# Three edits to a two-layer diffusion block on one core: where two half-matrix sums are rounded, when the late modulation chunks are made, and how the second-matrix tiles of the first MLP are cut into columns

## The reference, cut to what matters

```
def rms_norm(x, g, eps=1e-6):
    xf = x.astype(jnp.float32)
    y = xf * lax.rsqrt(jnp.mean(xf * xf, axis=-1, keepdims=True) + eps)
    return (y * g.astype(jnp.float32)).astype(x.dtype)

def modulate(x, g, shift, scale):
    return rms_norm(x, g) * (1.0 + scale) + shift

def squared_relu_mlp(h, w_in, w_out):
    return jnp.square(jax.nn.relu(h @ w_in)) @ w_out

for i in range(2):                       # DEPTH
    last = i == 1
    ml = jnp.split((silu(c) @ w_mod[i] + b_mod[i])[:, None, :], 6, axis=-1)
    mc = jnp.split(silu(c_ctx) @ w_mod[i] + b_mod[i], 6, axis=-1)
    hl = modulate(xl, norm_mix_g[i], ml[0], ml[1])
    hc = modulate(xc, norm_mix_g[i], mc[0], mc[1])
    # i == 0: Fourier groups + neighbourhood attention; i == 1: differential attention
    yl, yc = mixer_i(hl, hc)
    xl = xl + ml[2] * yl
    xl = xl + ml[5] * squared_relu_mlp(modulate(xl, norm_mlp_g[i], ml[3], ml[4]), w_mlp_in[i], w_mlp_out[i])
    if not last:                         # the context tokens go through the first layer's MLP only
        xc = xc + mc[2] * yc
        xc = xc + mc[5] * squared_relu_mlp(modulate(xc, norm_mlp_g[i], mc[3], mc[4]), w_mlp_in[i], w_mlp_out[i])
return rms_norm(xl, final_norm_g)
```

## Time and profile before

| | us |
|---|---|
| median of 3 runs | 1603.57 |
| lowest and highest run | 1601.69, 1603.67 |
| the profiled execution | 1603.09 |
| its span, first to last instruction | 1601.3 |
| PE busy | 1573.3 |
| DVE busy | 894.1 |
| ACT busy | 604.7 |
| POOL busy | 910.0 |

### The profile page before, as it was taken

The page is one execution under the profiler, slowest core; times in us unless marked ns, Lnnn a source line. Parts: engine busy times, 40 slices in busy tenths (PEclk is TensorE's granted clock), DMA queues, the critical chain, the costliest instruction groups (busy, mean ns, idle before and its releaser), DMA issues.

```text
span 1601.3 us, 24059 instructions
## 1 busy us (share of the span) xinstructions
PE 1573.3 (98%) x9272; PEld 1408.7 (88%) x9272; DVE 894.1 (56%) x1364; ACT 604.7 (38%) x1009; POOL 910.0 (57%) x1103
## 2 busy tenths in 40 slices
PE   8999999999899999999999999999999999999998
PEld 5889988988899999999998888878889878888887
DVE  4696457347845656647556746049965753232234
ACT  4422456325252342442542511248853412222222
POOL 2443475326677768768762656354415865555562
PEclk9999999999999999999999999999999999999999
DMA  8574212212042232333352223110003332323221
GB/s 350 197 268 153 93 41 100 80 48 85 27 157 81 80 119 82 116 115 123 105 182 82 91 78 96 66 43 1 1 12 130 129 126 93 105 92 101 83 93 53
DMA packets 50348, 163.15 MB, mean 102 GB/s; under 512 B 6336, under 2 KB 8768, under 8 KB 46656
## 3 DMA queue, kind: packets, MB, share of 16 engines
q1 hardware_dynamic: 50240, 161.68, 29.4%
HBM read 158.78 MB, written 2.10 MB: 100 GB/s over the span
## 4 chain that ended last, share of the span: by engine, by line
PE 86%; DVE 6%; POOL 2%; issue 2%; DMA 2%; ACT 1%; SPq 0%; POOLq 0%; DVEq 0%; ACTq 0%
PE ps L2109 24%; PE ps L2110 24%; PE ps L2111 24%; PE ps L2748 3%; PE ps L2710 2%; PE ps L2737 1%; PE ps L2615 1%; POOL w_lo L744 1%; PE ps L2603 1%; PE ps L2643 1%; PE ps L2427 1%; DVE mod_acc L1439 1%; DMA mod_big<-w_mod_dram 1%; DVE h L1562 1%; DMA raw<-units_dram 1%
## 5 line engine op out<-in xcount | busy, mean ns | idle before, releaser
L744 POOL TENSOR_TENSOR w_lo<-raw,w_hi 128x256 fp32r<-128x256 f32 x776 | 639.4, 856 | 492.4 <-ACT w_hi L949 362.0
L2109 PE MATMUL ps<-h,w_hi 128*128 128x512 f32 (+2 forms) x1016 | 358.0, 352 | 7.2 <-POOL w_lo L744 4.6
L2110 PE MATMUL ps<-h,w_lo 128*128 128x512 f32 (+2 forms) x1016 | 355.3, 350 | 0.0
L2111 PE MATMUL ps<-h,w_hi 128*128 128x512 f32 (+2 forms) x1016 | 355.0, 349 | 0.0
L2109 PEld LDWEIGHTS ps<-h,w_hi 128*128 128x128 f32 x1016 | 192.2, 189 | 32.3 <-issue 9.1
L2111 PEld LDWEIGHTS ps<-h,w_hi 128*128 128x128 f32 x1016 | 192.0, 189 | 17.1
L2110 PEld LDWEIGHTS ps<-h,w_lo 128*128 128x128 f32 x1016 | 192.2, 189 | 16.4
L1660 DVE SCALAR_TENSOR_TENSOR xl<-ps,mods,xl 128x384 f32<-128x384 f32 (+2 forms) x144 | 73.0, 539 | 210.8 <-PE ps L2111 209.0
L949 ACT ACTIVATE w_hi<-raw 128x1024 fp32r<-128x1024 f32 x120 | 126.4, 1054 | 113.2 <-PE ps L2111 107.7
L2109 PE MATMUL ps<-hidl,w_hi 128*128 128x384 f32 (+2 forms) x448 | 150.4, 336 | 2.5 <-DVE hidl L1704 1.5
L2110 PE MATMUL ps<-hidh,w_lo 128*128 128x384 f32 (+2 forms) x448 | 149.8, 334 | 0.0
(11 more groups left out here) (301 smaller groups left out, 3181.1 us busy)
## 6 DMA issues: line engine op xcount, KB each, us to landing
raw<-units_dram SPq DMA_DIRECT2D x187, 512.0 KB, 3.4
mod_ring<-w_mod_dram SPq DMA_DIRECT2D x96, 256.0 KB, 3.9
mod_big<-w_mod_dram SPq DMA_DIRECT2D x16, 1024.0 KB, 10.2
mod_late<-w_mod_dram SPq DMA_DIRECT2D x8, 1024.0 KB, 8.1
xl<-x_dram SPq DMA_DIRECT2D x2, 2048.0 KB, 8.3
bias<-bias_dram SPq DMA_DIRECT2D x8, 384.0 KB, 3.7
xc<-ctx_dram SPq DMA_DIRECT2D x2, 1024.0 KB, 10.4
out_dram<-out_t SPq DMA_DIRECT2D x16, 128.0 KB, 1.8
```

Of the source, the lines that this page charges most:

```text
L744: ins = nc.gpsimd.tensor_tensor(w_lo[:, s, sl], src[:, sl], w_hi[:, s, sl].bitcast(F32), op=ALU.subtract)
L2109: mm(out, a[0], b[1], start=start, stop=False, skip_group_check=onto)
L2110: mm(out, a[1], b[0], start=False, stop=False, skip_group_check=onto)
L2111: return mm(out, a[0], b[0], start=False, stop=stop, skip_group_check=onto)
```

## The change

It has three parts.

1. `turn_high(3)` (T4's rounding, ACT) stands behind the roundings of block 1's first three units; `turn_low(0)` (T1's low half, DVE) stands ahead of `add_tile(0, 2)` and of the second half of T2's sum, which goes behind that tile.
2. Modulation chunks 10 and 11 in the second MLP: PE's `mod_mm` one unit later each, DVE's steps of chunk 10 behind `hidden` 3 to 7 (one each, and the last four together), the extractions behind units 8 and 11, chunk 11's steps in groups of two, three and three, and SP's loads behind other units.
3. Tiles 2 to 7 of the second matrix in blocks 0 to 5 of the first MLP are cut into 512 + 256 columns instead of 384 + 384; DVE adds them with two instructions instead of three. Tiles 0 and 1 stay as they were.

```
-MOD_LATE = {6: (10, (4, 5)), 7: (10, (6, 7)), 8: (11, (0, 1)), 9: (11, (2, 3)), 11: (11, range(4, 8))}
+MOD_LATE = {7: (10, (4, 5)), 9: (10, (6, 7)), 10: (11, range(4)), 12: (11, range(4, 8))}
@@ ACT
                 turn_high(2, t3h[:], t3f[:])
-                turn_high(3, t4h[:], t4f[:])
...
                 next_block(1)
+                turn_high(3, t4h[:], t4f[:])
@@ DVE
-            def add_pieces(layer, par, i, m, count):
+            def add_pieces(layer, par, i, m, count, halves=True):
...
-                if layer == 0:
+                if layer == 0 and not halves:
+                    pieces += [(xc[:, i], 1, 1, slice(0, CTX))]
+                elif layer == 0:
...
-                    add_pieces(0, 2 + m % 2, m, 5, xa(0, b, m))
+                    add_pieces(0, 2 + m % 2, m, 5, xa(0, b, m), m < 2)
...
                 less(t2f[:], t1f[:], 1, 1, H1)
+                turn_low(0, h_lo[:, 0:4, H1], t1f[:], h_hi[:, 0:4, H1])
+                add_tile(0, 2)
                 join(t2f[:], half_f(1, 1, H1))
-                add_tile(0, 2)
-                turn_low(0, h_lo[:, 0:4, H1], t1f[:], h_hi[:, 0:4, H1])
                 add_tile(0, 3)
...
                             if first and i in (8, 12):
+                                extract_late(i // 4 + 8, 6)
                                 dve.wait_ge(mod_done, PE_MODS + i // 4 + 9)
...
                         if first:
-                            if 2 <= i < 6:
-                                mod_step(10, 2 * i - 4)
-                                mod_step(10, 2 * i - 3)
-                            elif i == 7:
-                                extract_late(10, 6)
-                            elif i in (8, 9):
-                                for k in range(4 * i - 32, 4 * i - 28):
-                                    mod_step(11, k)
-                            elif i == 10:
-                                extract_late(11, 6)
+                            for k in {3: (0,), 4: (1,), 5: (2,), 6: (3,), 7: (4, 5, 6, 7)}.get(i, ()):
+                                mod_step(10, k)
+                            for k in {8: (0, 1), 9: (2, 3, 4), 10: (5, 6, 7)}.get(i, ()):
+                                mod_step(11, k)
@@ PE
-                                cols = (H0, H1)[c]
-                                ins = three(ps[:, 4 + 2 * m + c, 0:EVEN], (w_hi[:, s, w], w_lo[:, s, w]),
+                                cols = ((H0, H1) if n == 0 else (slice(0, LAT), slice(LAT, TOK)))[c]
+                                ins = three(ps[:, 4 + 2 * m + c, 0:cols.stop - cols.start], (w_hi[:, s, w], w_lo[:, s, w]),
...
-                        if first and i in (7, 10):
-                            mod_mm(10 if i == 7 else 11, 6)
+                        if first and i in (8, 11):
+                            mod_mm(10 if i == 8 else 11, 6)
```

## The result

| | before | after |
|---|---|---|
| median, us (runs) | 1601.66 (20) | 1604.13 (20) |
| lowest and highest | 1600.33, 1603.67 | 1602.60, 1609.19 |
| the profiled execution | 1603.09 | 1602.95 |
| its span | 1601.3 | 1601.1 |

The change makes the kernel 2.47 us slower: ratio 1.0017, 95% interval 1.0011 to 1.0023, that is 1.8 to 3.7 us. That is within the 0.2% that the prediction counts as the same, and within its range. The 20 runs of before are those shown ahead and 17 more; the median of all 20 is 1.9 us under that of the first three.

What follows compares the result with a forecast made beforehand. PE's own pace and waits were taken to bound the kernel. Terms of -2.1, +1.6 and +0.4 gave -0.1 us, +2.4 with one clock fall of 2.5: 1605.5 us from 1603.09, range 1600.5 to 1608.5.

Steps and rivals of the forecast that it cites:

- Part 1, the wait moves from product 1 to product 2: First MLP, block 1: PE's wait before product 1 goes; one of 5.5 us stands before product 2.
- Part 1, the size: First MLP, block 1: product 2 starts at 443.15 instead of 445.26, a gain of 2.1 us.
- The bound of 5.1: First MLP, block 1: largest gain, in us, with nothing in POOL's way; product 2 then starts at 440.2.
- The clock: Behind the waits before product 2 and chunk 10's mod_mm: one fall to half clock in the two, costing 2.5 us.
- rival (b): Clock falls in both long waits, 2.7 us each: 1608.4 us, slower than before; chance 0.18.
- rival (a): No clock fall in either long wait: 1603.0 us; chance 0.20 shared with the case that nothing counts.
- Part 2, unit 8 waits for nothing and chunk 10's rows wait 5.06: Second MLP: the 0.92 us wait in unit 8 goes; PE waits 5.06 us before chunk 10's mod_mm.
- Part 2, chunk 11: Second MLP: with one DVE step less, 1.13 us, chunk 11 is 0.2 us late instead of 1.35.
- Part 3: First MLP, 36 tiles of 512 + 256 columns: width changes cost 0.4 us, bounds nothing and 1.8.
- The sum: Whole kernel: -2.1 + 1.6 + 0.4 = -0.1 us before the clock, +2.4 with one fall.
- Rival (c): First MLP: POOL's low 2 comes by 437.6, giving 1597.4 us, or 1599.9 with a fall; chance 0.14 including half-way form.
- (d): Nothing that counts changes, the first two parts cancel with shorter waits: 1603 us; chance 0.20 shared with no fall.

Runs made afterwards that it cites:

- E1: Kernel before with only part 1 of the change (T1's low half earlier, T4's rounding later): 1599.99 us, ratio 0.9989.
- E4: Kernel before plus part 1, with DVE's first four modulation steps in block 1 held until POOL made unit 2's low half: 1595.35 us, ratio 0.9963.
- E5: Whole change, with DVE's modulation steps in block 1 held until POOL made unit 2's low half: 1600.10 us, ratio 0.9985 against before.
- E2: Kernel before with only part 2 of the change (late modulation chunks one unit on): 1605.21 us, ratio 1.0026.
- E9: Whole change, with 256- and 512-column matmul triples alternating, eight width changes a tile instead of two: 1604.60 us, ratio 1.0015 against before.
- E6: Whole change, with 14 and 20 unread 512-column matmuls keeping PE at work in the two long waits: 1599.59 us, ratio 0.9986 against before.
- E3: Kernel before with only part 3 of the change (tiles 2 to 7 as 512 + 256 columns): 1602.39 us, ratio 1.0004.
- E7: Kernel before, with chunk 10's modulation steps moved earlier and chunk 11's steps and rows one unit later: 1597.73 us, ratio 0.9978.

## Why the prediction was right, and where it was not

The time and the class held: 1605.5 forecast, 1604.13 measured, and 1602.95 in the profiled execution, or 1604.9 with the 1.97 us of start-up that it was spared. The difference held better than the time, +2.4 forecast and +2.47 measured, since the forecast stood on an execution of 1603.09 and the median of 20 is 1601.66. That it is so near is in part luck, as the sum below shows. By its steps:

- **Part 1, the wait moves from product 1 to product 2**: right, and E1 shows it alone. Sum 1 was to start at 410.0; it starts at 408.03, 410.00 in the old count.
- **Part 1, the size**: mis-sized. Product 2 was forecast at 443.15 and starts at 439.37, 441.34 in the old count, 1.8 earlier; the move of the start is 3.9, not 2.1. The five groups to the end of low 1 took 429.61 - 408.03 = 21.6 us and not 22.8, and sum 4 and low 2, with what lies between, 9.66 and not 10.2. The wait is 3.84 instead of 5.5. The mechanism, a POOL piece against a DVE step, was right: E4 and E5 took the steps away and low 2 went from 4.59 to 2.81. The Trainium skill ("GPSIMD Engine Reference", section "Key points") names this contention with VectorE instructions that have two SBUF inputs, and the 4.59 and 2.81 agree with it. The bound of 5.1, the gain with T4's low half and no step in POOL's way, was too low: that is E4, where the wait is 2.6 us shorter than in E1, so the place can give 3.9 + 2.6 = 6.5.
- **The clock**: the step that failed as it was put. I took one fall in the two long waits at 2.5 us; in the profiled execution there were two of 1.6. The rival (b), that both waits fall, is the one whose mechanism came true there, so rival (a), no fall, is out; E2 and E5 show the late one again, E1 the first one again. E9 had the late one alone, so that the number of falls changes from run to run, as I had written, is right. (b)'s price of 2.7 each was too high for all six falls measured, 1.3 to 2.3. I had the price from 18 matmuls at half clock in the earlier trace rows, where the slow stretch was still on for 5.9 us after the wait. Behind the new waits of this execution PE ran 3.4 us at half clock, with 384-column matmuls 0.32 apart instead of 0.173: a loss of 1.6 each, 2 x 1.6 = 3.2 against 2.5 in the sum and 5.4 in (b). Behind product 2 this eats 1.6 of the 3.9.
- **The rule on the clock**: by the Trainium skill ("TensorE: Matmul & The Clock Gate", section "Part 1: The HAM clock gate") idleness gates the clock, which was (b)'s ground. E6 agrees: same waits, PE at work in them, granted clock 1.00 and no 0.43 us matmul. E9's wait of 3.76 us with a clock of 1.00 behind it shows that a wait of this length doesn't always meet a fall.
- **Part 2, unit 8 waits for nothing and chunk 10's rows wait 5.06**: right in mechanism and in size, 5.05. `hidden` 7 starts at 1276.26, 1279.83 in the old count (forecast 1279.80), and the split ends at 1285.77, 1289.34 (forecast 1289.3).
- **Part 2, chunk 11**: mis-sized, 0.63 and not 0.2. The subtraction of one step was right; what it was taken from, the 1.35 of the earlier trace rows, was the shortest such wait of all executions profiled. From the 1.75 of E1, E3 and E4 it is 1.75 - 1.13 = 0.62.
- **Part 3**: right that it costs and doesn't gain; 0.72 us instead of 0.4, inside the bounds of 0 and 1.8. The reason given (one change of width) is not borne out by E9: it is at most a third. The price was misread too: the 0.012 of the earlier trace rows is that of a group of three and three matmuls, which has two changes, and so has a tile.
- **The sum**: without the clock the forecast was -0.1; by the rows of after it is -3.9 + 2.0 + 0.7 = -1.2, and with two falls, 3.2, it is +2.0 where I had +2.4. An error of 1.8 at product 2 went one way; 0.7 for the falls, 0.4 for chunk 11 and 0.3 for the tiles went the other. The forecast was nearer than its terms: they cancelled, and that is luck.
- **Rival (c)**, low 2 by 437.6, did not come: it ends at 439.27, 441.24 in the old count. E4 comes nearer, by taking away the steps: low 2 ends at 436.33, which is 438.6 in the old count (E4's PE was 2.29 us ahead of before's ahead of this place), and PE still waits 1.37. **(d)** fell too: both places have their waits.
- **The marks of a wrong forecast** were not met: product 2 at 441.34 and not before 440.5, the split at 1289.34 and not before 1287.5, tiles of 4.18 and not over 4.2. The first and the last were near. Of the marks of a right one, the wait in front of product 2 was to be 5 to 6 us and is 3.84, the one in front of chunk 11's rows under 0.5 and is 0.63, and half clock stands behind both long waits instead of one.

## What to carry over

When a wait is removed, follow the list of the engine that ended it: its next item is late by what it still shares with its neighbour, and moving that neighbour, steps that nobody waits for, gave more than the edit itself. Side work is to be ready before the main engine's turn, so move it up into gaps ahead of it before moving the turn back: the one direction cost 3.3 us here, the other, with chunk 11 one unit later, gave 4.2. Read a price such as a wait in front of one instruction from several executions, since one can be short by 0.4 us and a start-up by 2, and look at every run's granted clock before you take a profiled execution for a typical one.

## What the hardware showed that I had not expected

- One DVE instruction of 1.90 us beside four POOL pieces makes them 4.12 us instead of 2.81 (E4); T4's low half and the steps after it, beside eight pieces, make 9.5 of what would be 5.6.
- A wait of 3.84 us (the change) and one of 3.94 (E1) were followed by half clock, one of 3.76 (E9) was not: its windows from 439 to 442 us have 1.00. Those of 4.75 (before, E2, E3, E7) and of 5.05 (the change, E2, E5, E9) all were. The stretch at half clock behind a wait is 3.4 us in the change's two places; behind the 5.05 it is 2.8 in E9 and 5.0 in E5, behind the 4.75 it is 5.9 in before and 4.6 in E3.
- The half clock at 20 to 28 us, in a stretch that no edit touched, came in some executions and not in others; it is worth about 2 us, as much as the change. E7's profiled execution has one of 3.4 us at 105 us that no other has.
